# Where the fill matmuls stand in the SSD loop: whole fills per chunk, none between the first two segments

## The reference

```
xbc = silu(causal_depthwise_conv(xbc, conv_w, conv_b))          # 4 taps
xs, bm, cm = split(xbc)                                         # 4 groups of 8 heads, 64 wide; state 128
a_cum = cumsum(dt * a)                                          # inside a chunk of 128 tokens
decay[l, s] = exp(a_cum[l] - a_cum[s]) for s <= l, else 0
y_diag = (cm bm^T * decay) (xs dt)                              # inside the chunk
state_k = state_(k-1) * exp(a_cum[end]) + bm^T (decay_to_end xs dt)
y_off = exp(a_cum) * (cm state_(k-1))                           # from the chunks before
y = (y_diag + y_off + xs * d_skip) * silu(z), normalised per group
```

## Time and profile before

| | |
|---|---|
| median of 3 runs | 2513.49 us (2513.4 to 2515.33) |
| profiled execution | 2513.4 us, its span 2511.7 us |
| busy: TensorE, VectorE, ScalarE, GpSimd | 94%, 55%, 29%, 34% of the span |
| mean granted TensorE clock | 0.98 of full |
| group loops | about 870 to 1380 us of the span |

### The profile page before, as it was taken

How to read it: one execution, slowest core, us unless ns; L and a number is a source line. 1 busy time by engine, 2 the same in 40 slices (tenths; PEclk the granted TensorE clock), 3 DMA queues, 4 the chain that set the end, 5 groups by cost and what they waited for, 6 DMA issues and landing times.

```text
span 2511.7 us, 31936 instructions
## 1 busy us (share of the span) xinstructions
PE 2371.1 (94%) x12062; PEld 1940.4 (77%) x12062; DVE 1381.0 (55%) x1971; ACT 727.7 (29%) x1373; POOL 863.5 (34%) x353
## 2 busy tenths in 40 slices
PE   3999999997998999999998999999799999999997
PEld 3966878884556988888886788888688888888885
DVE  4249999973666267585766565554523132222316
ACT  5154121004552233434364211025421111212112
POOL 1221322325773262544443222345232223333221
PEclk8999999998999999999998999999999999999998
DMA  7110242215562113131221543323211111111103
GB/s 263 34 34 30 99 174 100 100 51 192 184 202 76 34 60 126 39 114 67 85 97 55 184 168 134 117 101 136 84 36 49 50 50 50 50 42 41 50 34 134
DMA packets 145737, 233.92 MB, mean 93 GB/s; under 512 B 8068, under 2 KB 111844, under 8 KB 144612
## 3 DMA queue, kind: packets, MB, share of 16 engines
q1 hardware_dynamic: 121952, 173.45, 20.8%
q10 hardware_dynamic: 23684, 59.06, 6.1%
HBM read 180.06 MB, written 52.43 MB: 93 GB/s over the span
## 4 chain that ended last, share of the span: by engine, by line
PE 86%; DVE 6%; ACT 3%; issue 3%; DMA 1%; POOL 0%; ACTq 0%; SPq 0%; DVEq 0%
PE ps L637 84%; DVE c_out L1800 1%; PE ps L841 1%; DVE probT L1743 1%; DVE mod_sum L1588 1%; PE ps L924 0%; DMA ada_raw<-in_ada_w_dram 0%; DVE x_tm L1970 0%; PE ps L861 0%; DMA x_d<-x_tm 0%; ACT decay L1437 0%; DVE x_tm L1907 0%; ACT h_tmp L1138 0%; PE ps L682 0%; DVE x_tm L1932 0%
## 5 line engine op out<-in xcount | busy, mean ns | idle before, releaser
L637 PE MATMUL ps<-a_hi,w_hi 128*128 128x512 f32 x1728 | 677.2, 392 | 11.5 <-DVE a_lo L1853 5.6
L637 PE MATMUL ps<-a_lo,w_hi 128*128 128x512 f32 x1728 | 674.6, 390 | 0.0
L571 POOL CAST w_hi<-raw 128x2048 fp32r<-128x2048 f32 x90 | 176.1, 1957 | 1311.7 <-PE ps L637 1014.5
L637 PE MATMUL ps<-a_hi,w_lo 128*128 128x512 f32 x1728 | 544.2, 390 | 0.0
L573 POOL TENSOR_TENSOR w_lo<-raw,w_hi 128x2048 fp32r<-128x2048 f32 x90 | 432.4, 4805 | 7.2
L1932 DVE TENSOR_TENSOR x_tm<-x_tm,ps 128x1024 f32<-128x1024 f32 x120 | 146.5, 1221 | 453.2 <-PE ps L637 453.2
L637 PEld LDWEIGHTS ps<-a_hi,w_hi 128*128 128x128 f32 x1728 | 325.8, 189 | 80.9 <-issue 7.1
L637 PEld LDWEIGHTS ps<-a_hi,w_lo 128*128 128x128 f32 x1728 | 325.5, 188 | 68.3
L637 PEld LDWEIGHTS ps<-a_lo,w_hi 128*128 128x128 f32 x1728 | 325.7, 188 | 66.8
L637 PE MATMUL ps<-w_hi,a_hi 128*128 128x256 f32 (+1 forms) x896 | 259.3, 289 | 5.0 <-ACT row L1489 2.0
L637 PE MATMUL ps<-w_lo,a_hi 128*128 128x256 f32 (+1 forms) x896 | 253.2, 283 | 0.0
(11 more groups left out here) (249 smaller groups left out, 3166.4 us busy)
## 6 DMA issues: line engine op xcount, KB each, us to landing
raw<-in_w_in_dram SPq DMA_DIRECT2D x35, 1024.0 KB, 5.2
ada_raw<-in_ada_w_dram SPq DMA_DIRECT2D x16, 1024.0 KB, 8.7
raw<-in_w_up_dram SPq DMA_DIRECT2D x16, 1024.0 KB, 5.7
raw<-in_w_down_dram SPq DMA_DIRECT2D x16, 1024.0 KB, 4.7
gates<-gate_d SPq DMA_DIRECT2D x12, 1024.0 KB, 4.9
act_raw<-acts_d ACTq DMA_DIRECT2D x20, 512.0 KB, 6.1
ada<-in_ada_w_dram SPq DMA_DIRECT2D x8, 1024.0 KB, 20.8
acts_d<-decay ACTq DMA_DIRECT2D x16, 512.0 KB, 3.1
```

Source lines behind the costliest of these rows:

```text
L571: nc.gpsimd.tensor_copy(hi, src).then_inc(hi_made, 1)
L637: return nc.tensor.matmul(o, a, b, start=start, stop=stop)
```

## The change

The table of halves becomes a table of whole fills. In group 0 no fill stands between the first segments any more, and fill `k` stands in chunk `k`. In groups 1 to 3 `segments(0)` and `segments(1)` follow each other, both halves of fill 1 come behind them, and fills 2 to 7 stand in chunks 0, 1, 3, 4, 5 and 6; chunks 2 and 7 carry none. This holds for group 3 too, whose chunks 0 to 5 carried them. ScalarE's evacuations are moved to match, each two chunks behind its fill.

```
-        def fill_parts(g, k):
-            first = 2 if g == 0 else 4
-            each = (2, 2, 2, 2, 2, 2, 1, 1) if g == 0 else (2, 2, 2, 2, 1, 1, 1, 1) if g + 1 < NG else (2, 2, 2, 2, 2, 2, 0, 0)
-            n = first + sum(each[0:k])
-            return range(n, n + each[k])
+        def fill_places(g):
+            return {k: k for k in range(NT)} if g == 0 else {0: 2, 1: 3, 3: 4, 4: 5, 5: 6, 6: 7}
...
-                j = 1 if g else 0
                 segments(0)
-                fill(g, j, 0)
                 segments(1)
-                fill(g, j, 1)
+                if g:
+                    fill(g, 1, 0)
+                    fill(g, 1, 1)
                 pe.wait_ge(tile_out, g * 5 + 5)
+                places = fill_places(g)
                 for k in range(NT):
...
-                    for part in fill_parts(g, k):
-                        fill(g, *divmod(part, 2))
+                    if k in places:
+                        fill(g, places[k], 0)
+                        fill(g, places[k], 1)
...
-                    if k == 1:
-                        fill_evac(g, 1 if g else 0)
-                    for part in fill_parts(g, k - 2) if k >= 2 else ():
-                        if part % 2:
-                            fill_evac(g, part // 2)
+                    if k == 1 and g:
+                        fill_evac(g, 1)
+                    if k - 2 in places:
+                        fill_evac(g, places[k - 2])
```

## The result

The changed kernel took 2542.67 us in the median of 4 runs (2539.17 to 2546.9), the kernel before 2513.44. The ratio is 1.0117 with a 95% interval of 1.0099 to 1.0136: 1.2% slower, 29.2 us. The forecast was slower by 20.0 us, 2533.4, range 2525.5 to 2542.5. The profiled execution took 2542.98 us with a span of 2541.3.

A forecast was written before the change was run, and what follows sets the result against it. TensorE, busy 94% of the span, was taken to bound the kernel. Idle-time terms summed to 16.2 us, plus 3.8 for the clock: 20.0 us on 2513.4, giving 2533.4 us, range 2525.5 to 2542.5.

The forecast's parts named there:

- TensorE bounds the kernel, the rest is idle time: TensorE is busy 94% of the span, so new idle time there lengthens the result unless something later was waiting anyway.
- The starts, 8.9 + 3.7 us of waits: Group starts, `decay` ready no earlier: 2.96 us lost in each of groups 1 to 3, 8.9 together; group 0 loses 3.7.
- Chunk 3, +7.4 us: Groups 1 to 3, chunk 2 without its fill: chunk 3's state matmul waits 2.45 us for `zy` each, +7.4 us.
- Chunk 5 and the end of group 3, -1.9 and -4.7 us: Chunk 5's `zy` waits in groups 1 and 2 go, -1.9 us; group 3 chunk 7's wait and half clock go, -4.7.
- The x transposes, 2.8 us: Before `turn_tile(4)` in groups 2 and 3: the convolution chain comes later against TensorE, 1.4 us of new wait each, +2.8.
- The clock, 3.8 us: Seven candidate stalls at group starts and chunk 3: two falls to half clock counted at 1.9 us each, +3.8 us.
- at most 4.99 us under work: Longest time the granted clock was said to stay at 0.50 under work, from 1391.21 after another stall.
- The second case: Clock falls in all seven stalls at the group starts and chunk 3: 28.7 us slower, 2542.1 us; chance 0.14.
- The rule that was weighed: The skill's HAM oscillation rule: bursts behind recurring waits begin at half clock; for all seven stalls, the second case, 2542.1 us.

The follow-up runs named there:

- the starts alone: Against the kernel before, only the group starts changed (no fill between the first two segments, group 0 whole fills), chunks of groups 1 to 3 as before: 2535.41 us.
- The kernel whose clock stays full through the loops: The changed kernel plus unread matmuls in seven waits, 13 at each group's start and 9 in chunk 3 of groups 1 to 3: 2531.01 us.
- the last experiment: The kernel before with the starts' whole fill between the first two segments and halves spread 2, 2, 1, 1, 2, 2, 1, 1 in groups 1 to 3: 2508.8 us.

## Why the prediction was right and wrong

- **TensorE bounds the kernel, the rest is idle time.** Right. Nothing in the run took up the waits later.
- **The starts, 8.9 + 3.7 us of waits.** Right. `decay` stands 5.19 us behind the first segment as before; the starts alone cost 22 us, of which 12.6 are these terms (the 3.7 of group 0 is a fill that was moved, less an earlier mix). The kernel whose clock stays full through the loops bears the whole sum out: it costs 17.6 us, where 16.2 were forecast without the clock. The waits for `decay` read 3.00 us each, not the 3.7, 3.7, 3.7 and 4.6 named, because segment 1's first matmul and a wait for `cb` of 0.4 us, which the prediction doesn't have, lie in the same gap; in group 3 the segment before it ran at half clock and took some of the gap as well.
- **Chunk 3, +7.4 us.** Right: 2.4 us where 2.45 stood, in groups 1 and 2 of the changed kernel.
- **Chunk 5 and the end of group 3, -1.9 and -4.7 us.** Right: the first is gone (1.1 us each by the starts of the state matmuls), the end gained 4.6.
- **The x transposes, 2.8 us.** Right in kind and place, somewhat small: waits of 1.46 and 2.01 us. Group 3 had 0.06 us of room (1288.19 to 1288.25 in the kernel before), not the 0.36 that was read in group 2 and taken for both.
- **The clock, 3.8 us. This step failed**, and by it the total: by the ledger it should have been 12.8, for six falls of 2.1 us on average in place of two of 1.9. The argument that "the 3.7 us are shorter than the time for which the clock held in a longer stall" looked at the clock during a stall, as if a stall that ends with full clock had cost nothing. In groups 1 and 2 the clock was still full when TensorE resumed, and fell 0.8 to 0.9 us later, for some 3 us of the fill. And where it fell, it often cost more than the 1.9 us taken: 3.3 us in group 0, where the mix and two chunks' segments ran slowly, 3.1 in chunk 3 of group 3. The earlier trace rows stop where each stall stops. The trace of the kernel before had the counterexample, outside the group loops; these are the first matmul behind a stall of 3.92 us, and the windows of the stall and of the work behind it:

```profile
597.78 1.00 PE L637 MATMUL ps<-ones,ada_sum 128*128 128x1 f32 x4 [3.92 <-POOL ada_sum L591]
...
593.90:597.59 3.69, 0.00 (x0) 0.00 (x0) 1.46 (x4) 3.36 (x6) 3.53 (x4) 1.00 0.00 0
597.78:604.40 6.62, 6.62 (x19) 4.80 (x19) 0.25 (x1) 0.59 (x1) 6.46 (x3) 0.50 0.47 158
```

The stall was at full clock for all but its last 0.2 us, and 6.6 us of work behind it were at half. So the "at most 4.99 us under work" of the prediction is wrong for its own trace; by its own rule, half of such a stretch, this fall cost up to 3.3 us and not 1.9.

- **The second case** (all seven fall, 28.7 us, 2542.1) was nearest to the measured time and had been given 0.14. That it comes so near is luck in part: five of the seven fell, another did that it doesn't have, and their sizes run from 1.2 to 3.3 us.
- **The rule that was weighed.** I had set it aside for the waits of 3.7 us and all but one of the waits of 2.3. The Trainium skill ("TensorE: Matmul & The Clock Gate", the section on HAM oscillation) has each burst behind a wait begin slowly. This case's runs agree with it in the sum, with 14 us between the kernel with idle waits and the one with busy waits. They differ in the place: in groups 1 and 2 the burst began at full clock and lost it after 0.8 to 0.9 us.
- **The range.** Its upper end, 2542.5, lies 0.4 us above the second case, as if seven falls at 1.9 us were the worst; a fall of 3.3 us has no room in it.

What stays open: when the clock falls. All twelve waits of 3.00 us for `decay`, in three executions, had a fall in or behind them. Waits of 1.73, 1.92, 2.01, 2.20 and 2.38 us had one in some execution; waits of 1.46, 1.73, 1.92, 2.00, 2.20 and 2.38 us held in others. The same wait brought a fall in one execution and none in the next (2.0 us at group 3's x transposes). Why chunk 3 fell in three groups of one kernel and in one of another was not tried.

## What to carry to other kernels

A wait newly opened on a matmul engine that was never idle has two prices, its length and the stretch at half clock that follows, and here the second was nearly as large as the first. Look for it behind the wait too, not in it alone, and do so at every stall of the trace at hand before a change is forecast. Independent work should go into the gap that is longest in front of a known chain, and in pieces that cover that chain's length, instead of being laid down evenly. Where one execution's clock decides several microseconds, a range has to reach past the sum in which every wait has its fall, since a fall can cost more than the single row at hand.

## What the runs showed of the hardware

Behind some waits of 1.9 to 3.0 us, during which it had read 1.00 throughout, the granted clock fell from 1.00 to 0.50 only 0.1 to 2.3 us after TensorE had resumed (0.83 us in group 1 of the changed kernel); at others it fell in the last 0.04 to 1.7 us of the wait. In the changed kernel's loops it then read 0.50 for 3.4 to 10.2 us. 79 matmuls of 0.21 us with a result that nobody reads, laid into seven such waits, made the kernel 14 us faster than without them. 32 in place of 79 were worth 6 to 8 us. In the last experiment VectorE's first operation on the state took 5.08 us in place of 0.69 while GpSimd split a weight block.
